# Eight expert tiles of gates to a memory row, in place of four, in a two-layer attention and expert kernel

## The chip, the cores and the metric

The kernel runs on one core of a Trainium2 chip. The metric is the device time of one execution in microseconds (us). TensorE is PE in the rows, its weight loads PEld, VectorE is DVE, ScalarE is ACT, GpSimd is POOL, and SyncE, which only issues transfers here, is SP.

## The reference

Two layers over 512 tokens of width 1024, all in float32: attention with compressed keys and values in the first, a gated linear recurrence in the second, and after each a mixture of 16384 small experts. The change lies in the experts, which are, for each block of 128 tokens:

```python
q = (xt @ w_q).reshape(PEER_TBLOCK, PEER_HEADS, 2, PEER_HALF)
s = jnp.einsum('thpd,hpnd->thpn', q, sub_keys).astype(jnp.float32)
s1, i1 = lax.top_k(s[:, :, 0], PEER_TOPK)
s2, i2 = lax.top_k(s[:, :, 1], PEER_TOPK)
...
top, pos = lax.top_k(cand, PEER_TOPK)
eidx = jnp.take_along_axis(cidx, pos, axis=-1)
gates = jax.nn.softmax(top, axis=-1)
act = jax.nn.gelu(jnp.einsum('td,thkd->thk', xt, u[eidx]).astype(jnp.float32), approximate=False)
return jnp.einsum('thk,thkd->td', (gates * act).astype(xt.dtype), v[eidx])
```

Every token takes 128 experts (8 heads, 16 each) out of 128 x 128.

## The kernel before

**Dense and gathered tokens.** For 384 of the 512 tokens (`D`) the experts are computed densely: all 16384 of them, in 128 tiles of 128 experts, with a gate that is zero wherever a token did not choose the expert. For the last 128 tokens (`FAR`) the chosen rows of `u` and `v` are gathered one expert a token at a time: 128 gathers of 512 KB from `u` and 128 from `v` a layer, issued by GpSimd (line 616) into six buffers, and used by VectorE in `far_dot` (line 1337) and `far_add` (line 1353). A gather waits until the row six before it has been used.

**The u phase.** Step `s` of 0 to 127 multiplies tile `u[s]` with the tokens on TensorE: 24 matmuls of 384 columns (8 pieces of the width, each as three products of a high and a low part). ScalarE takes the bank through Gelu into one of four buffers `act_st` (line 849), and SP stores it into `acts_dram` (192 KB, line 545). Gelu of tile c waits until the store of tile c - 4 has landed. The four weight buffers are filled by SP (line 514), ScalarE rounds a tile to its high part (line 679), and VectorE makes the low part (line 1330). SP issues the load of a tile once the low part of the tile four before it is made.

**The gates.** From step 41 to 118 TensorE also makes the gates of the dense tokens from one-hot factors, four tokens (a quad) at a time. ScalarE moves them (line 857) into one of two buffers `gate_st` of 32 tokens each, and `store_gates` (line 550) writes such a buffer, 2 MB, into `gates_dram`: 12 stores a layer. The array in memory is `gates_dram[GG, P, HALVES, GF, HALF_TOK]`: `GF` expert tiles lie together, and a row that is stored in one piece holds `GF` tiles x 32 tokens. The last store of a layer goes out at about step 116.

**The v phase.** Step c of 0 to 127 multiplies the product of activation and gate with tile `v[c]`: 18 matmuls of 512 columns. SP loads the activations back (192 KB a tile, line 559), and the gates of `GF` tiles in one transfer, `load_gates` (line 565), into one of two buffers. VectorE multiplies both (`make_product`, line 1364), ScalarE rounds the product to its high part (line 875), VectorE makes its low part (`product_low`, line 1370), and TensorE waits for that.

**What sets the order.** The program is written by hand as one list for each engine, and each engine runs its list in order. All of SP's transfers go into one queue (q1), the gathers into another (q0). On SP the two first gate loads stand at step 127, ahead of the first four `v` tiles and of the stores of activations 120 to 127:

```python
                    if s == NKEYS - 1:
                        for b in range(2):
                            sp.wait_ge(gate_stored[b], 16 * (HALVES // 2) * (layer + 1))
                        load_gates(0)
                        load_gates(1)
                    for c in range(act_loads_before(s), act_loads_before(s + 1)):
                        if c % GF == 2 and 1 <= c // GF < GG - 1:
                            load_gates(c // GF + 1)
                        load_act(c)
```

On ScalarE `product_high(0)`, the step before TensorE's first `v` matmul, stands in step 125, behind `gelu(125)` and the rounding of tile `v[1]`. So the end of the u phase and the start of the v phase are linked through the landing of the store of activations 121.

Of the kernel before, what the change touches and what calls it, by code (L numbers as in the profile page):

```python
# [43 lines left out]
RING = 4  # L44
APART = 2
AFTER_VALUES = (TT - 1, *range(TT - 1))
GF = 4
GG = NKEYS // GF
DENSE_T = TT - 1
D = DENSE_T * P  # L50
# [90 lines left out]
def act_loads_before(step):  # L141


    return min(max(min(2 * (step - NKEYS + 3), ACTS_EARLY), step - NKEYS, 0), NKEYS)
# [161 lines left out]
def model(nc, x, pos, consts, masks, gains, fgain, frows, mla_t, hg_t, pq_t, keys_t, u_t, u_rows, v_t, out):  # L306
    jobs = plan()
    ctx = ExitStack()
    with ctx:
# [5 lines left out]
        def sem(name):  # L315
            if name not in sems:
                sems[name] = ctx.enter_context(nc.semaphore(name))
            return sems[name]


        acts_dram = nc.dram_tensor("acts_dram", [NKEYS, P, D], F32, kind="Internal").ap()
        gates_dram = nc.dram_tensor("gates_dram", [GG, P, HALVES, GF, HALF_TOK], F32, kind="Internal").ap()

# [29 lines left out]
        def cut(offset, *shape):  # L353
            n = int(np.prod(shape))
            ap = arena[:, offset:offset + n]
            if len(shape) == 1:
                return ap
            names = "abcd"[:len(shape)]
            return ap.rearrange(f"p ({' '.join(names)}) -> p {' '.join(names)}", **dict(zip(names, shape)))
# [15 lines left out]
        keysT = cut(0, 16, NKEYS)  # L375
        gate_st = cut(3072, 2, GG, GF, HALF_TOK)
        gate_ld = cut(3072, 2, HALVES, GF, HALF_TOK)
        cand = cut(3072, HEADS, STAIRS)
# [130 lines left out]
        def _(sp):  # L509
# [20 lines left out]
            def experts(layer):  # L530
# [30 lines left out]
                def load_gates(g):  # L561

                    if g >= 2:
                        sp.wait_ge(sem("product_made"), NKEYS * layer + GF * (g - 1))
                    sp.dma_start(gate_ld[:, g % 2].rearrange("p h f t -> p (h f t)"),
                                 gates_dram[g].rearrange("p h f t -> p (h f t)")).then_inc(gate_loaded[g % 2], 16)

                stored = 0
                for s in range(2 * NKEYS + 8):
# [14 lines left out]
# [3 lines that stand above are left out]
# [1436 lines left out]
```

## Time and profile before

| | us |
|---|---|
| median of 3 runs | 2978.71 |
| lowest and highest | 2976.94, 2978.97 |
| the profiled execution | 2975.47 |
| its span, first to last instruction | 2973.7 |
| TensorE busy | 2941.9 (99%) |
| VectorE busy | 2364.5 (80%) |
| ScalarE, GpSimd busy | 1197.0, 1284.2 |
| DMA | 799.76 MB, mean 269 GB/s |

The layers' expert phases take 325 to 1425 us and 1865 to 2960 us of the span. The granted TensorE clock has a mean of 0.997. The transfers are read in two ways: as the rate of a stretch (GB/s), and as the share that each queue's packets take of the 16 DMA engines. The share can exceed 100%, since packets of one engine overlap; so a cost is worked out from the rate. A chain of waits is followed back from the last instruction of a stretch to whatever released it, and its rows tell what sets the end of that stretch.

### The profile page before, as it was taken

How to read it: one execution, taken by the hardware profiler on the slowest of the kernel's cores; microseconds unless marked ns; L12 is line 12 of the kernel's file. 1: busy time of each engine (PE TensorE's matmuls, PEld its weight loads, DVE VectorE, ACT ScalarE, POOL GpSimd, SP SyncE). 2: the span in 40 equal slices, each digit the busy share in tenths (PEclk: the TensorE clock that was granted, in tenths of full speed). 3: DMA queues.
4: the chain of work that ended last, by engine and by line, in shares of the span. 5: the costliest groups of instructions: out<-in, count | busy, mean ns of one | idle time of the engine just before them, and what ended most of it. 6: DMA issues, size and time to landing. Idle time of an engine off the chain costs nothing.

```text
span 2973.7 us, 43852 instructions
## 1 busy us (share of the span) xinstructions
PE 2941.9 (99%) x16072; PEld 2620.6 (88%) x16072; DVE 2364.5 (80%) x4442; ACT 1197.0 (40%) x1881; POOL 1284.2 (43%) x747
## 2 busy tenths in 40 slices
PE   8999999999999999999999999999999999999999
PEld 7578999999998888888889888999999998888887
DVE  7547999899978888888256637999898968888887
ACT  5543333444433333333435633334444433333333
POOL 4133565434434444442447433655344444444441
PEclk9999999999999999999999999999999999999999
DMA  4022468999999999998221022559999999999995
GB/s 153 32 80 97 129 200 303 352 374 375 368 378 396 365 366 357 362 360 295 100 92 43 30 94 85 181 174 346 365 361 381 364 385 397 360 361 365 358 363 213
DMA packets 345572, 799.76 MB, mean 269 GB/s; under 512 B 27920, under 2 KB 192016, under 8 KB 345104
## 3 DMA queue, kind: packets, MB, share of 16 engines
q1 hardware_dynamic: 271488, 528.44, 50.7%
q0 software_dynamic: 73728, 268.47, 23.6%
q8 instruction: 129, 2.11, 0.3%
q14 instruction: 83, 0.68, 0.1%
q10 hardware_dynamic: 144, 0.07, 0.0%
HBM read 694.10 MB, written 102.76 MB: 268 GB/s over the span
## 4 chain that ended last, share of the span: by engine, by line
PE 96%; DVE 1%; ACT 1%; DMA 1%; issue 0%; POOL 0%; SPq 0%; DVEq 0%; ACTq 0%
PE PS L1583 29%; PE PS L1585 29%; PE PS L1584 29%; PE PS L1789 3%; PE PS L1860 1%; PE PS L1766 1%; PE PS L1697 1%; DMA acts_dram<-arena 1%; DVE resid L1086 1%; PE PS L1696 1%; PE PS L1743 1%; ACT arena L692 0%; PE PS L1731 0%; ACT w_hi L679 0%; POOL w_lo L605 0%
## 5 line engine op out<-in xcount | busy, mean ns | idle before, releaser
L679 ACT ACTIVATE w_hi<-w_raw 128x1024 fp32r<-128x1024 f32 x607 | 641.0, 1057 | 697.1 <-PE PS L1585 652.0
L1583 PE MATMUL PS<-x_hi,w_hi 128*128 128x384 f32 (+1 forms) x2596 | 910.4, 351 | 6.3 <-POOL w_lo L605 4.9
L1585 PE MATMUL PS<-x_hi,w_lo 128*128 128x384 f32 (+1 forms) x2596 | 899.3, 346 | 0.0
L1584 PE MATMUL PS<-x_lo,w_hi 128*128 128x384 f32 (+1 forms) x2596 | 897.9, 346 | 0.0
L1583 PE MATMUL PS<-w_hi,x_hi 128*128 128x512 f32 x1744 | 680.0, 390 | 1.6 <-DVE x_lo L1370 0.8
L1584 PE MATMUL PS<-w_lo,x_hi 128*128 128x512 f32 x1744 | 678.9, 389 | 0.0
L1585 PE MATMUL PS<-w_hi,x_lo 128*128 128x512 f32 x1744 | 678.8, 389 | 0.0
L616 POOL DMA_INDIRECT arena<-in_v_t,arena x256 | 428.6, 1674 | 557.1 <-DVE resid L1353 520.5
L605 POOL TENSOR_TENSOR w_lo<-w_raw,w_hi 128x1024 fp32r<-128x1024 f32 x167 | 412.6, 2474 | 536.4 <-ACT w_hi L679 536.3
L1330 DVE TENSOR_TENSOR w_lo<-w_raw,w_hi 128x1024 fp32r<-128x1024 f32 x440 | 537.1, 1221 | 101.6 <-ACT w_hi L679 98.4
L616 POOL DMA_INDIRECT arena<-in_u_rows,arena x256 | 373.4, 1458 | 499.9 <-DVE arena L1337 446.2
L1583 PEld LDWEIGHTS PS<-x_hi,w_hi 128*128 128x128 f32 x2596 | 487.9, 188 | 26.8 <-issue 6.3
L1585 PEld LDWEIGHTS PS<-x_hi,w_lo 128*128 128x128 f32 x2596 | 487.5, 188 | 22.4
L1584 PEld LDWEIGHTS PS<-x_lo,w_hi 128*128 128x128 f32 x2596 | 488.1, 188 | 19.2 <-issue 0.2
L849 ACT ACTIVATE arena<-PS 128x384 f32<-128x384 f32 x256 | 125.9, 492 | 692.5 <-PE PS L1585 495.2
L1583 PEld LDWEIGHTS PS<-w_hi,x_hi 128*128 128x128 f32 x1744 | 327.7, 188 | 71.0 <-issue 3.0
L1585 PEld LDWEIGHTS PS<-w_hi,x_lo 128*128 128x128 f32 x1744 | 327.7, 188 | 68.1
L1584 PEld LDWEIGHTS PS<-w_lo,x_hi 128*128 128x128 f32 x1744 | 327.7, 188 | 67.8
L1353 DVE SCALAR_TENSOR_TENSOR resid<-arena,resid 128x1024 f32<-128x1024 f32 x256 | 327.5, 1279 | 1.3
L1337 DVE SCALAR_TENSOR_TENSOR arena<-arena 128x1024 f32<-128x1024 f32 x256 | 307.2, 1219 | 0.4
L1370 DVE TENSOR_TENSOR x_lo<-arena,x_hi 128x384 fp32r<-128x384 f32 x256 | 144.7, 565 | 163.1 <-ACT x_hi L875 155.8
L1364 DVE TENSOR_TENSOR arena<-arena 128x384 f32<-128x384 f32 x256 | 141.3, 552 | 3.7 <-DMA arena<-acts_dram 3.7
(187 smaller groups left out, 2321.4 us busy)
## 6 DMA issues: line engine op xcount, KB each, us to landing
w_raw<-in_u_t SPq DMA_DIRECT2D x256, 512.0 KB
w_raw<-in_v_t SPq DMA_DIRECT2D x256, 512.0 KB
acts_dram<-arena SPq DMA_DIRECT2D x256, 192.0 KB
gates_dram<-arena SPq DMA_DIRECT2D x24, 2048.0 KB
arena<-acts_dram SPq DMA_DIRECT2D x256, 192.0 KB
arena<-gates_dram SPq DMA_DIRECT2D x64, 768.0 KB
w_raw<-in_hg_t SPq DMA_DIRECT2D x40, 512.0 KB
w_raw<-in_pq_t SPq DMA_DIRECT2D x32, 512.0 KB
```

Source lines behind the costliest of these rows:

```text
L605: pool.tensor_tensor(w_lo[:, n % RING, :], w_raw[:, n % RING, :], f32(w_hi[:, n % RING, :]), ALU.subtract).then_inc(pool_low, 1)
L616: pool.indirect_dma_start(row[k % ROWS], None, u_at if k < HK else v_at, bass.IndirectOffsetOnAxis(ap=at, axis=0))\
L679: act.activation(w_hi[:, slot, :], w_raw[:, slot, :], ACT.Copy).then_inc(hi_ready, 1)
L849: act.activation(act_st[:, c % RING, :], PS[:, c % 4, 0:D], ACT.Gelu).then_inc(gelu_done, 1)
L1330: dve.tensor_tensor(w_lo[:, n % RING, :], w_raw[:, n % RING, :], f32(w_hi[:, n % RING, :]), ALU.subtract).then_inc(dve_low, 1)
L1337: dve.scalar_tensor_tensor(r, r, 1.0, far_x, ALU.mult, ALU.mult, accum_out=far_act[:, k:k + 1]).then_inc(sem("dotted"), 1)
L1353: dve.scalar_tensor_tensor(resid[:, FAR, :], r, far_w[:, k:k + 1], resid[:, FAR, :], ALU.mult, ALU.add).then_inc(sem("far_added"), 1)
L1364: dve.tensor_tensor(product[:, c % RING, :].rearrange(tokens, t=HALF_TOK), act_ld[:, c % RING, :].rearrange(tokens, t=HALF_TOK), gate_ld[: ...
L1370: dve.tensor_tensor(product_at(x_lo, c), product[:, c % RING, :].rearrange("p (t n) -> p t n", n=P), product_at(f32(x_hi), c), ALU.subtrac ...
L1583: pe.matmul(ps, wh, xh, start=start, stop=False)
L1584: pe.matmul(ps, wh, xl, start=False, stop=False)
L1585: return pe.matmul(ps, wl, xh, start=False, stop=stop)
```

## The change

`GF` becomes 8, and so `GG` 16.

```diff
-GF = 4
+GF = 8
 GG = NKEYS // GF
```

A store of gates still moves 2 MB, now in 2048 rows of 1 KB in place of 4096 of 512 bytes. A load of gates brings 8 tiles: 1.5 MB in place of 768 KB, with 12 KB a partition in place of 6 KB, and there are 32 loads in place of 64. Each of the two load buffers grows from 1536 to 3072 words a partition; they lie over the store buffers, which are free by then. The loads that follow the first two stand every 8 tiles in place of every 4, six steps ahead of their first use in place of two. The lists of TensorE, VectorE, ScalarE and GpSimd have the same rows as before; only SP's differs.

SP's list at the end of the first layer's u phase, before (`w_raw` are the weight buffers, `arena` holds all others):

```order
L545 DMA acts_dram<-arena 128x384
L565 DMA arena<-gates_dram 128x1536 x2
L514 DMA w_raw<-in_v_t 128x1024
L545 DMA acts_dram<-arena 128x384
L514 DMA w_raw<-in_v_t 128x1024
L545 DMA acts_dram<-arena 128x384
```

And with the change:

```order
L545 DMA acts_dram<-arena 128x384
L565 DMA arena<-gates_dram 128x3072 x2
L514 DMA w_raw<-in_v_t 128x1024
L545 DMA acts_dram<-arena 128x384
L514 DMA w_raw<-in_v_t 128x1024
L545 DMA acts_dram<-arena 128x384
```

Nothing moved here, but the two transfers ahead of the `v` tiles and the stores are twice as large.

SP's list a few steps into the v phase, before:

```order
L565 DMA arena<-gates_dram 128x1536
L559 DMA arena<-acts_dram 128x384
L514 DMA w_raw<-in_v_t 128x1024
L545 DMA acts_dram<-arena 128x384
L559 DMA arena<-acts_dram 128x384
L514 DMA w_raw<-in_v_t 128x1024
L559 DMA arena<-acts_dram 128x384
L514 DMA w_raw<-in_v_t 128x1024
L559 DMA arena<-acts_dram 128x384
L514 DMA w_raw<-in_v_t 128x1024
L565 DMA arena<-gates_dram 128x1536
```

And with the change, from the load of activations 9 on:

```order
L559 DMA arena<-acts_dram 128x384
L514 DMA w_raw<-in_v_t 128x1024
L565 DMA arena<-gates_dram 128x3072
L559 DMA arena<-acts_dram 128x384
L514 DMA w_raw<-in_v_t 128x1024
L559 DMA arena<-acts_dram 128x384
L514 DMA w_raw<-in_v_t 128x1024
```

The load of gates that stood at tile 6 is gone, and one of twice its size stands where that of tile 10 was; the next follows eight tiles later.

## Rows read from the trace of the kernel before

**Rows 1.** The page: busy us and share of each engine, and the chain's shares

```profile
PE 2941.9 (99%) x16072; PEld 2620.6 (88%) x16072; DVE 2364.5 (80%) x4442; ACT 1197.0 (40%) x1881; POOL 1284.2 (43%) x747
PE 96%; DVE 1%; ACT 1%; DMA 1%; issue 0%; POOL 0%; SPq 0%; DVEq 0%; ACTq 0%
```

**Rows 2.** Who waited for whom, TensorE: us in total, times, longest

```profile
PE PS L1641 <- DVE arena L1056: 9.1, 3, 8.3
PE PS L1583 <- DVE x_lo L1370: 0.8, 1, 0.8
```

**Rows 3.** Chain of waits at the second layer's phase change: start, us, what

```profile
2427.88 13.19 DMA acts_dram<-arena
...
2441.54 1.05 ACT w_hi L679
2442.59 0.42 ACT x_hi L875
...
2443.03 0.57 DVE x_lo L1370
```

**Rows 4.** Timeline of the first layer's phase change: ScalarE, VectorE, TensorE

```profile
899.38 0.49 ACT L849 ACTIVATE arena<-PS 128x384 f32<-128x384 f32 x1 [2.80 <-DMA acts_dram<-arena]
900.71 0.51 ACT L875 ACTIVATE x_hi<-arena 128x384 fp32r<-128x384 f32 x1
901.26 0.56 DVE L1370 TENSOR_TENSOR x_lo<-arena,x_hi 128x384 fp32r<-128x384 f32 x1 [3.43 <-ACT x_hi L875]
901.75 0.34 PE L1585 MATMUL PS<-x_hi,w_lo 128*128 128x384 f32 x1
901.96 0.47 PE L1583 MATMUL PS<-w_hi,x_hi 128*128 128x512 f32 x1
```

**Rows 5.** SP's timeline, second layer: gate store, tile behind it, gate loads

```profile
2400.06 0.37 SPq L550 DMA_DIRECT2D gates_dram<-arena  x1
2400.47 13.15 SPq L514 DMA_DIRECT2D w_raw<-in_u_t  x1
...
2419.27 0.89 SPq L565 DMA_DIRECT2D arena<-gates_dram  x2
```

**Rows 6.** By stretch: us, busy us of each engine, granted clock, DMA share, GB/s

```profile
882.00:892.00 10.00, 10.00 (x59) 10.00 (x59) 9.10 (x14) 2.92 (x5) 7.63 (x5) 1.00 1.03 415
2434.00:2444.00 10.00, 9.19 (x53) 8.90 (x52) 2.98 (x6) 3.29 (x5) 2.54 (x2) 1.00 1.03 413
2485.00:2940.00 455.00, 455.00 (x2009) 376.87 (x2008) 382.56 (x455) 164.92 (x224) 190.96 (x114) 1.00 0.97 360
```

**Rows 7.** Transfers of 885 to 886.5 us, nearly all a load of gates

```profile
DMA packets 120, 0.64 MB, mean 430 GB/s; under 512 B 14, under 2 KB 15, under 8 KB 120
```

**Rows 8.** Transfers of 867 to 868 us, all of them a store of gates

```profile
DMA packets 677, 0.35 MB, mean 347 GB/s; under 512 B 0, under 2 KB 677, under 8 KB 677
```

**Rows 9.** Queues of 2430 to 2441 us: packets, MB, share of 16 engines

```profile
q0 software_dynamic: 676, 2.51, 55.8%
q1 hardware_dynamic: 812, 2.04, 46.8%
```

**Rows 10.** Gathers' queue in 899 to 903 us, then in 2441 to 2445 us

```profile
q0 software_dynamic: 94, 0.32, 19.6%
...
q0 software_dynamic: 187, 0.64, 39.2%
```

**Rows 11.** ScalarE and VectorE at the first load of gates within the v phase

```profile
923.40 1.06 ACT L679 ACTIVATE w_hi<-w_raw 128x1024 fp32r<-128x1024 f32 x1 [5.75 <-DMA w_raw<-in_v_t]
...
915.90 0.55 DVE L1364 TENSOR_TENSOR arena<-arena 128x384 f32<-128x384 f32 x1
...
920.66 0.56 DVE L1364 TENSOR_TENSOR arena<-arena 128x384 f32<-128x384 f32 x1 [1.18 <-DMA arena<-acts_dram]
...
924.90 0.56 DVE L1370 TENSOR_TENSOR x_lo<-arena,x_hi 128x384 fp32r<-128x384 f32 x1 [1.36 <-ACT x_hi L875]
925.38 0.56 DVE L1364 TENSOR_TENSOR arena<-arena 128x384 f32<-128x384 f32 x1
```

## The prediction, on record before the change was run

> **What bounds the kernel now.** I read the page first. TensorE is busy for 99% of the span, and the chain that ended last is 96% TensorE [rows 1]. An edit that touches only SP's transfers can therefore act in two ways alone: it removes one of TensorE's few waits, or it makes a new one. The list of TensorE's waits says how much there is to remove: the largest entry belongs to the norms, and the only one that hangs on the gates or activations is a single wait of 0.8 us for the low part of a product [rows 2]. So the gain has a ceiling of about 1 us, whatever the change does for the transfers. The rest of the question is where a slower or later transfer would reach TensorE.
>
> The second view is the chain of waits around that one wait. It stands at the change from the u phase to the v phase of the second layer, and the reader is to see its largest link: the store of activations 121, issued at 2427.88 us, lands 13.19 us later; then come the rounding of the tile `v[1]` (1.05 us), `product_high(0)` and `product_low(0)`, and then TensorE's first `v` matmul [rows 3]. A store of 192 KB does not need 13 us by itself: it stands in a queue. In the first layer the same sequence ends just in time. Gelu of tile 125 starts at 899.38 us after a wait for a store, `product_high(0)` at 900.71, `product_low(0)` runs from 901.26 to 901.82, and TensorE, whose last u matmul starts at 901.75, starts the `v` matmuls at 901.96 [rows 4]. At the 0.17 us from one u matmul to the next (59 in 10 us [rows 6]) 901.92 would have been possible, and the low part was ready at 901.82: about 0.1 us of slack. So in both layers the landing of that store sets the start of the v phase, with 0.1 us and no slack.
>
> The third view is the table by stretches. From the last store of gates to the start of the v phase the DMA engines are full: shares of 1.03 and 413 to 415 GB/s [rows 6]. In such a stretch every byte that is put ahead of the store delays it.
>
> **The change part by part.**
>
> *Larger first loads.* On SP the two first gate loads are issued at 2419.27 us [rows 5], ahead of the store of activations 121, in one queue. They grow from 2 x 0.786 MB to 2 x 1.573 MB. While such a load had the engines nearly alone it ran at 430 GB/s [rows 7], so the 1.573 MB that come on top take 1.573 / 0.430 = 3.7 us a layer. They bring the gates of tiles 8 to 15, which nobody wants for another 30 us. At the 413 GB/s of the full stretch [rows 6] it would be 3.8; I take 3.7, since the two ends lie so close.
>
> *Larger rows of the stores.* In a stretch that holds nothing but 512-byte rows the rate is 347 GB/s [rows 8]. The 2.097 MB of a store take 6.0 us at that rate, and would take 4.9 us at the 430 GB/s of the large rows [rows 7]. No row shows 1 KB; so the saving lies between 0 and 1.1 us a store. If the difference is a fixed cost per packet, it halves when the packets halve, and half of 1.1 us, some 0.5 us, is my value. Of the 12 stores of a layer only the last one counts: TensorE waited for none of the others, and it stands ahead of the critical store in the same full queue. So -0.5 us a layer (0 to -1.1).
>
> The Trainium skill, page "DMA: Bandwidth & Descriptors", section "Specifications", gives 512 B as the smallest transfer that reaches line rate; by that rule alone the longer rows save nothing, and the sum below would be 1 us higher. The trace does not agree: 347 against 430 GB/s [rows 7, 8].
>
> *The gathers take their turns.* The queue of the gathers runs beside SP's. From 2430 to 2441 us it took 55.8% of the engines, and SP's queue 46.8% [rows 9]: while gathers are pending, SP's transfers get less than half. But there are only six gathers in flight until VectorE has used the next row, and VectorE is held there by `product_low(0)` itself. What of them had not run when the critical store landed, can now run before it: 0.32 MB after 899 us in the first layer and 0.64 MB after 2441 us in the second [rows 10], which is 0.8 and 1.5 us at 415 GB/s [rows 6]. The bound below is nothing, if the store keeps its place ahead of them. With shares of 56 to 47 the extra 3.2 us of SP's queue leave room for all of it, so I take 0.8 and 1.5.
>
> The same page, section "Queues, rings and completion order", says that each DMA engine goes round-robin between the queues that have work for it. By that rule the full amounts hold, and the shares of [rows 9] agree with it; without it the sum would be 2.3 us lower.
>
> *SP is free earlier.* Behind the last store of gates SP needs 13.15 us to issue one weight tile [rows 5]; half as many descriptors should shorten that. I cost it at nothing, because the transfers behind it go through a queue that is never empty from there on: an earlier place at the issuing end changes no landing. If it did, the first rival below would hold.
>
> *The later loads.* Half as many loads, twice the size, six steps ahead of use in place of two. The first one within the v phase moves from tile 6 to tile 10. In the profile the one at tile 6 has cost VectorE's cadence: the products start 4.8 and 4.7 us apart there (915.90, 920.66, 925.38), where TensorE takes 4.08 us a tile (455 us over 2009 matmuls, 18 a tile [rows 6]), and ScalarE waited 5.75 us for a weight tile [rows 11]. TensorE did not wait. Its tile 6 was due at 901.96 + 6 x 4.08 = 926.4 us, and the low part of that product was ready at 925.5 [rows 4, 11]. Without this load the margin can grow for four more tiles at the pace of the other steps. So the move is worth nothing to TensorE, and the doubled load at tile 10 meets a larger margin; I cost it at 0, with an upper bound in the second rival. Over the rest of the phase the bytes are the same, at 360 GB/s against the 430 that the engines reach.
>
> *The sum.* First layer: 3.7 - 0.5 + 0.8 = 4.0 us later for the critical store, less 0.1 us of slack, 3.9. Second layer: 3.7 - 0.5 + 1.5 = 4.7, all of it a wait, since there the 0.8 us stand already. Behind the store nothing changes. 3.9 + 4.7 = +8.6 us. The profiled execution took 2975.47 us, so it would take 2984.1; the median of the runs shown is 3.2 us above the profiled one, and the forecast on that scale is 2978.71 + 8.6 = 2987.3, say **2987 us**. The step needs TensorE's two waits at the phase change to be worth their length alone, and the clock to stay: it is granted at 1.00 in the stretch with the wait of 0.8 us [rows 6].
>
> The unknown terms give this case a range of its own: all low (stores save 1.1, no gathers) 3.9 - 0.6 - 0.8 = 2.5 and 4.7 - 0.6 - 1.5 = 2.6, so +5.1; all high (stores save nothing) +9.6. That is 2984 to 2988.
>
> **The rivals.**
>
> *The landing is bound by issue, not by bytes.* If the long block on SP is what makes the stores of activations 116 and onward late, halving the descriptors shortens the block from 13.15 to about 6.6 us, more than the 3.7 us that the loads add. Then the critical store lands no later, and the 0.8 us wait goes away. For it speaks the size of the block [rows 5]; against it speak the full engines in every later stretch [rows 6]. It decides if the engines show gaps between the last gate store and the first gate load. The time would be 2975.5 - 0.8, or 2978 on the scale of the median, and at the most 2 us above it: not slower.
>
> *Bytes only.* The store keeps its place against the gathers. Then the sum is 3.7 - 0.5 - 0.1 + 3.7 - 0.5 = +6.3 us, 2985, and with cheaper 1 KB rows +5.1. The shares of [rows 9] speak against it.
>
> *The bursts stall TensorE as well.* The load at tile 6 cost about 1.5 us of margin (4.8 and 4.7 us in place of 4.08, twice). One of twice the size costs 3 us and, with the gathers' turns, up to 6; the margin at tile 10 will be some 4 to 6 us. If it is short, 1 to 2 us a layer come on top, and if it recurs at tile 18 the same again: +10.5 to +16, say 2991. For it speaks the wait of 5.75 us [rows 11]; against it the steady phase with 0.97 share and no wait on TensorE [rows 2, 6].
>
> That the change does not do what it says can be left out: SP's list shows it.
>
> **How the numbers follow.** The forecast has 0.57, the bound by issue 0.17, bytes only 0.14, the bursts 0.12. A measurement of this kernel can tell about 0.2%, 6 us, from no change. The forecast's own range begins at +5.1, so 0.10 of its 0.57 count as within 6 us; of the bound by issue 0.14 do, and 0.03 count as faster, for a gain that I have not seen; of bytes only 0.08 do. Slower by over 0.2%: 0.47 + 0.06 + 0.12 = 0.65. Within 0.2%: 0.10 + 0.14 + 0.08 = 0.32. Faster: 0.03. The range leaves out most of the bound by issue below and the worst bursts above: 2979.5 to 2993.
>
> **What would show it.** TensorE's waits: the entry for the low part of a product (line 1370) should stand at two waits, near 4 and 5.5 us, in place of one of 0.8. The chain before each should hold a store of activations that lands some 16 to 18 us after its issue. SP's block behind a gate store should be shorter with no effect on TensorE, and the rate within a gate store should rise from 347 to about 380 GB/s. In the v phase TensorE should have no wait. The forecast is wrong if Gelu of tile 125 starts within 1 us of its place relative to TensorE's last u matmul, if the gathers run only after the store, or if waits appear at tiles 11 or 12.

## The result, and the profile after

The changed kernel takes 2985.49 us in the median of 10 runs (2982.04 to 2987.59), the kernel before 2977.49 us (2972.51 to 2979.97). The ratio is 1.0024, with a 95% interval of 1.0015 to 1.0033: slower by 8.0 us, where +8.6 was forecast. The profiled execution has a span of 2985.0 us, against 2973.7. These two lie further apart than the medians: the changed kernel's took 2986.81 us, and that of the kernel before, with 2975.47 us, was the fastest of its three.

The list of TensorE's waits, after (us in total, times, longest); the second row answers to the same one in [rows 2]:

```profile
PE PS L1641 <- DVE arena L1056: 9.1, 3, 8.3
PE PS L1583 <- DVE x_lo L1370: 8.1, 2, 4.3
```

The wait for the low part of product 0 was one of 0.8 us, and is two of 3.8 and 4.3. The chain of waits before the second one (start, us, what) answers to [rows 3]:

```profile
2428.64 21.01 DMA acts_dram<-arena
...
2450.11 1.05 ACT w_hi L679
2451.16 0.42 ACT x_hi L875
...
2451.60 0.57 DVE x_lo L1370
```

The links behind the store have the lengths that they had; the store of activations 121 lands 21.0 us after its issue in place of 13.2. Counted from the issue of the last gate store, it was issued 3.1 us sooner (24.8 in place of 27.8 us) and landed 4.8 us later (45.8 in place of 41.0). SP's timeline over the same change of phase, second layer, answers to [rows 5]:

```profile
2403.88 0.37 SPq L550 DMA_DIRECT2D gates_dram<-arena  x1
2404.29 6.73 SPq L514 DMA_DIRECT2D w_raw<-in_u_t  x1
...
2419.55 2.75 SPq L565 DMA_DIRECT2D arena<-gates_dram  x2
```

SP is held for 6.7 us behind the gate store in place of 13.2, and that has not helped. What decides is seen when all bytes are counted from the issue of the last gate store to the start of Gelu of tile 125, which waits for the critical store. Second layer, before (2400.1 to 2441.2 us) and after (2403.9 to 2449.7): all transfers, and SP's queue alone.

```profile
DMA packets 8821, 16.28 MB, mean 396 GB/s; under 512 B 530, under 2 KB 6014, under 8 KB 8819
...
q1 hardware_dynamic: 7102, 9.96, 65.2%
```

```profile
DMA packets 6955, 18.49 MB, mean 404 GB/s; under 512 B 557, under 2 KB 3991, under 8 KB 6697
...
q1 hardware_dynamic: 5079, 11.64, 64.8%
```

A mean rate is bytes over time, so that the two fit together proves nothing by itself. What the count shows is that the engines were no slower in the longer stretch (404 GB/s in place of 396): it is longer because more bytes passed in it. The 2.21 MB more would take 5.6 us at 396 GB/s, and the higher rate gives 0.9 us of them back: 4.7 us. Of the 2.21 MB, SP's queue carries 1.68, of which 1.57 are the larger first loads, and the gathers' queue 0.54 (6.28 and 6.82 MB). The first layer, from 857.9 to 899.4 us before and from 859.1 to 904.5 us after, shows the same in sum:

```profile
DMA packets 8737, 16.25 MB, mean 392 GB/s; under 512 B 520, under 2 KB 5898, under 8 KB 8734
DMA packets 6960, 18.49 MB, mean 407 GB/s; under 512 B 564, under 2 KB 3998, under 8 KB 6701
```

There the 2.24 MB more would be 5.7 us, and the higher rate gives 1.7 back.

There is a second thing in the profile that the prediction had not reckoned with. The stretches at both changes of phase, after (columns as in [rows 6]; the granted clock stands third from the end):

```profile
904.00:909.00 5.00, 1.89 (x7) 1.56 (x8) 2.60 (x5) 4.06 (x8) 0.16 (x1) 0.95 0.99 387
909.00:914.00 5.00, 5.00 (x17) 4.00 (x16) 5.00 (x9) 2.35 (x4) 3.20 (x2) 0.71 0.70 225
2447.00:2452.00 5.00, 1.05 (x7) 0.73 (x5) 1.58 (x2) 2.27 (x5) 0.00 (x0) 0.93 1.04 413
2452.00:2459.00 7.00, 6.69 (x17) 5.36 (x18) 7.00 (x12) 3.20 (x5) 3.36 (x2) 0.56 0.71 236
2459.00:2465.00 6.00, 6.00 (x28) 4.94 (x27) 6.00 (x9) 2.98 (x5) 3.04 (x3) 1.00 1.01 338
```

Right behind each wait the granted clock falls from 2.4 to 1.2 GHz for part of the stretch: from 2452 to 2459 us TensorE starts 17 matmuls in 7 us, where 28 fit into the 6 us after. At the level of the last row, 7 us hold 33, so this stretch lost about 3.4 us of work, and the one at 909 us about 1.4 (17 matmuls in 5 us, where 23 would fit). In the profile the change thus costs 7.3 us of waits and some 5 us of half clock, together somewhat more than the 11.3 us between the spans; the half clock that both kernels have in other stretches is not the same in the two executions either.

### The profile page after: what moved, and what is told of

It reads as the page before. It is cut to its first block, busy times and chain, and to the rows that moved or that the text cites. A ratio compares the mean times of both kernels' runs of the same rounds, so it can differ in the third digit from the quotient of the medians.

```text
span 2985.0 us, 43820 instructions
## 1 busy us (share of the span) xinstructions
PE 2946.8 (99%) x16072; PEld 2624.1 (88%) x16072; DVE 2365.9 (79%) x4442; ACT 1196.8 (40%) x1881; POOL 1256.4 (42%) x747
## 4 chain that ended last, share of the span: by engine, by line
PE 94%; DMA 2%; DVE 1%; ACT 1%; issue 0%; POOL 0%; SPq 0%; DVEq 0%; ACTq 0%
PE PS L1583 28%; PE PS L1585 28%; PE PS L1584 28%; PE PS L1789 3%; DMA acts_dram<-arena 2%; PE PS L1860 1%; PE PS L1766 1%; PE PS L1697 1%; DVE resid L1086 1%; PE PS L1696 1%; PE PS L1743 1%; ACT arena L692 0%; PE PS L1731 0%; ACT w_hi L679 0%; PE PS L1887 0%
## 5 line engine op out<-in xcount | busy, mean ns | idle before, releaser
L616 POOL DMA_INDIRECT arena<-in_u_rows,arena x256 | 346.9, 1355 | 519.5 <-DVE arena L1337 468.5
```

Source lines behind the costliest of these rows:

```text
L616: pool.indirect_dma_start(row[k % ROWS], None, u_at if k < HK else v_at, bass.IndirectOffsetOnAxis(ap=at, axis=0))\
```

## The experiments

The times of one version spread by 4 to 14 us, and those of the kernel before by 13 to 20 in a group of runs. Each ratio is to the kernel before on the same chip. Where an edit adds lines, the line numbers shift by 1 to 6.

**The second load later.** From the changed kernel:

```diff
                         load_gates(0)
+                    if s == NKEYS + 3:
                         load_gates(1)
```

> The changed kernel, with the second of the two first gate loads issued three steps later, behind the stores of activations 120 to 123. My theory (the change costs what the bytes ahead of the critical store take in a full queue): ahead of that store now stands one load of 1.57 MB, as many bytes as two loads did before the change, and the last gate store is some 0.5 us shorter. So TensorE's wait for the low part of a product falls from 8.1 us in two waits to at most 0.5 us in all, no stretch at half clock stands behind the phase change, and the ratio to the kernel before is 0.9995 to 1.0002. Rival (the larger loads cost by themselves, wherever they stand: 12 KB packets, or the later bursts of 1.5 MB): the waits stay at 4 us or more and the ratio at 1.002 or above.

2974.64 us, ratio 0.998 (0.9971 to 0.9989). TensorE has no wait for a product in the profile. The same count of bytes as above, for this kernel, 2399.3 to 2438.6 us of the second layer:

```profile
DMA packets 6515, 15.81 MB, mean 402 GB/s; under 512 B 510, under 2 KB 3954, under 8 KB 6385
...
q1 hardware_dynamic: 4923, 10.00, 65.5%
```

SP's queue has 1.64 MB fewer than the changed kernel, the gathers 1.0 MB fewer (5.78 against 6.82), at about the same rate, and the stretch is 39.3 us long. The rival falls: the larger loads cost nothing by themselves, only where they stand. I had forecast 0.9995 to 1.0002; the kernel is faster than that, and than the kernel before beyond the interval; a second profile of the kernel before (the last experiment) shows a part of what it had to gain.

**The same edit to the kernel before:**

> The kernel before, with only the second first gate load (768 KB) issued three steps later. My theory: 0.79 MB fewer ahead of the critical store, 1.8 us, which takes away the wait of 0.8 us in the second layer and leaves TensorE about 1 us of slack at both phase changes. No wait on the low part of a product, ratio 0.9995 to 1.0000. Rival (the phase change is set by the issue on SP or by the gate store alone): the wait of 0.8 us stays.

2975.50 us, ratio 0.9986 (0.9976 to 0.9995). No wait for a product, as expected. The gain is larger than the 0.9995 to 1.0000 that was forecast, here too. It has other waits, though, 2.1 us at the gates' matmuls.

**The loads without the stores.** Memory as before (`GF` = 4), but each load takes two groups:

```diff
-                    sp.dma_start(gate_ld[:, g % 2].rearrange("p h f t -> p (h f t)"),
-                                 gates_dram[g].rearrange("p h f t -> p (h f t)")).then_inc(gate_loaded[g % 2], 16)
+                    sp.dma_start(gate_ld[:, 2 * b:2 * b + 2].rearrange("p g h f t -> p g (h f t)"),
+                                 gates_dram[2 * g:2 * g + 2].rearrange("g p h f t -> p g (h f t)"))\
+                        .then_inc(gate_loaded[b], 16)
```

> The loads of the change without its stores: the gates lie in memory as before (rows of 512 bytes stored), and each load brings two groups of four tiles, 1.5 MB with two pieces of 6 KB a partition, at the same places in SP's list as in the changed kernel. My theory: the same bytes ahead of the critical store, and a gate store that is 0.5 us longer in each layer, so the two waits sum to 8.5 to 10 us and the ratio is 1.0025 to 1.0035. Rival (the 12 KB rows of the loads, or the 1 KB rows of the stores, are what costs): waits below 4 us and a ratio below 1.0015.

2990.85 us, ratio 1.0036 (1.0023 to 1.0049). The wait, and the bytes from 2406.5 to 2454.6 us:

```profile
PE PS L1587 <- DVE x_lo L1374: 13.0, 2, 6.5
```

```profile
DMA packets 9431, 18.90 MB, mean 393 GB/s; under 512 B 579, under 2 KB 6147, under 8 KB 9428
...
q1 hardware_dynamic: 7546, 12.02, 66.4%
```

So the loads alone bring more waits than the whole change does, 13.0 against 8.1 us, where I had expected 8.5 to 10. The intervals of the two ratios overlap (1.0015 to 1.0033 for the change), but the same pair with the gathers held (below) is apart beyond its intervals. The longer rows of the stores thus give back about 5 us of waits, where I had put 0.5 us a layer on them. One other thing differs between the two kernels, the pieces of the loads, 6 KB here and 12 KB in the changed kernel. While they moved beside gathers the rates were 430 GB/s (2436 to 2438 us here) and 436 (2431 to 2435 us of the changed kernel), which is 0.1 us over the 3.15 MB of two loads. The rate during a store is what I took it for: one microsecond that holds nothing but 1 KB rows (2414 to 2415 us of the changed kernel) ran at 386 GB/s, between the 347 and 430 of [rows 7, 8], which makes 6.0 - 5.4 = 0.6 us a store.

```profile
DMA packets 377, 0.39 MB, mean 386 GB/s; under 512 B 0, under 2 KB 377, under 8 KB 377
```

The rest of the gap is taken up below.

**The gathers held.** From the changed kernel, on GpSimd ahead of the first gather of `v` rows:

```diff
+                    if k == HK:
+                        pool.wait_ge(sem("product_low"), NKEYS * layer + 1)
                     at = row_at[:, k % HK:k % HK + 1]
```

> The changed kernel, with the first gather of a v row of each layer (and with it all later ones) held until the low part of product 0 is made. It tests the term for the gathers' turns. If three of the six gathers beside the critical store no longer run before it, it lands up to 3 x 1.26 = 3.8 us earlier, and at the least the 0.8 and 1.5 us of my sum come back: the two waits sum to 1 to 6 us, the ratio is 1.0005 to 1.0018. Rival (SP's queue keeps its place, the gathers take nothing from it): the waits stay at 8.1 us. The held gathers might make VectorE late for the rows behind the phase change; TensorE has 4 us a tile there, and I expect no wait from it.

2975.85 us, ratio 0.998 (0.9971 to 0.9990). The waits for the low parts are four, 1.4 us in all, as expected (1 to 6 us); the ratio is better than the 1.0005 to 1.0018 forecast, as with the second load late. From 2399.2 to 2441.2 us:

```profile
DMA packets 6517, 16.90 MB, mean 402 GB/s; under 512 B 508, under 2 KB 3939, under 8 KB 6259
...
q1 hardware_dynamic: 5070, 11.62, 70.5%
```

SP's queue carries what it does in the changed kernel (11.62 and 11.64 MB), and the gathers 5.25 in place of 6.82 MB. The difference is 1.57 MB, three gathers of 0.524 MB: those that were held. At 402 GB/s that is 3.9 us, and the stretch is 3.8 us shorter. In the changed kernel three gathers of `v` rows were issued at 2433.3, 2438.3 and 2440.3 us, while the critical store stood in its queue (2428.6 to 2449.7 us). All three had run ahead of it, so the gathers' turns are as real as I assumed them, and a gather that runs early costs its full length.

**The changed kernel again,** beside the next three:

> The changed kernel once more, on the same chip as the three runs of this group, for comparison with them and for a second profile: the times of single executions spread over 5 to 14 us. If the wait at the phase change is what the change costs, the two waits for the low part of product 0 should again sum to 6 to 10 us, with a stretch at half the granted clock behind each, and the ratio to the kernel before should be 1.0015 to 1.003.

2984.32 us (2981.84 to 2990.02), ratio 1.0016 (1.0007 to 1.0025). Two waits, 8.2 us, and again a granted clock of 0.58 and 0.56 in the 7 us behind them.

**Both edits together:**

> The changed kernel with both: the second first gate load three steps later, and the gathers of v rows held until the low part of product 0. Each alone has brought TensorE's waits at the phase change from 8.1 to 0 and 1.4 us and the time to 0.998 of the kernel before. My theory: with no wait left to remove, the two do not add up; ratio 0.9975 to 0.9990, the low part of product 0 done 2 us or more earlier than with either, and no half clock there. Rival (each removes a cost of its own elsewhere, say in the bursts of the v phase): the gains add up to 0.997 or less.

2974.60 us, ratio 0.9986 (0.9977 to 0.9994). No wait, and no gain beyond either edit alone: the low part of product 0 is ready 4 us earlier than with the gathers held alone, and 1 to 2 us earlier than with the second load late alone (2 or more were expected), and TensorE has no use for it.

**The wait filled.** Into TensorE's list between the last u tile and the first v tile:

```diff
+                for _ in range(15):
+                    pe.matmul(PS[:, 7, 0:P], ident, iota, start=True, stop=True)
```

> The changed kernel, with 15 small float32 matmuls of constants (3 to 4 us, into a bank that the first v matmul overwrites) put into TensorE's list between the last u tile and the first v tile, where it waits 3.8 and 4.3 us. Theory of the clock: the half clock seen right behind these waits (3.4 and 6.8 us long, some 5 us of time) comes from TensorE's idle time before it; with the wait filled it does not occur, the fill costs nothing as long as it is shorter than the wait, and the time falls by 2 to 5 us against the changed kernel, ratio 1.000 to 1.0015. Rival (the clock falls there for another reason, or at random): the half clock stays behind the phase changes and the time is that of the changed kernel or up to 2 us above it, ratio 1.002 to 1.0035.

2983.84 us (2980.45 to 2984.32), ratio 1.0016 (1.0007 to 1.0025). The stretches of the phase changes in its profile, first and second layer:

```profile
904.00:908.00 4.00, 4.00 (x35) 3.85 (x33) 0.58 (x2) 1.95 (x4) 0.00 (x0) 1.00 1.04 410
908.00:914.00 6.00, 5.67 (x26) 4.67 (x26) 6.00 (x10) 4.67 (x7) 2.35 (x2) 1.00 0.71 245
2447.00:2451.00 4.00, 4.00 (x35) 4.00 (x34) 0.98 (x1) 1.48 (x3) 0.00 (x0) 1.00 1.03 410
2451.00:2458.00 7.00, 6.38 (x31) 5.22 (x30) 6.60 (x12) 5.18 (x9) 2.62 (x2) 1.00 0.72 258
```

With the wait filled by work that nobody needs, the clock stays at 2.4 GHz, so in the profile the half clock does come from TensorE's idle time. The spans differ by 6.2 us (2982.0, against 2988.2 for the changed kernel of this group), but the latter is that of the slowest of its 11 executions. The medians are only 0.5 us apart, where I had expected 2 to 5, and the ratios are the same. What the fill changes is the upper end, 2984.3 in place of 2990.0. The mean granted clock of each execution says more than one profile: it is 0.997 or above in all 11 with the fill, and 0.995 or 0.996 in 5 of 11 without it, and these 5 are the slowest, 2984.5 us and more. Over the 11 the clock averages 0.9971 and 0.9964, which is 2.1 us of 2984 (an estimate, from clocks given to three digits), and the mean times are 2983.0 and 2984.8 us. So the half clock costs about 2 us on average, not 5, though with this spread the times alone do not show it. The third kernel of the group fits: the kernel with both edits, which has no wait, has a mean of 2974.6 us, 8.4 us below the filled kernel, and TensorE's waits or their fill are 8.2 us.

**The double loads with the gathers held.** It asks where the 5 us between the two layouts come from.

> The loads of the change without its stores (rows of 512 bytes as before), with the gathers of v rows held until the low part of product 0. Without the hold this kernel waited 13.0 us in the two phase changes and the changed kernel 8.1 us: 2.4 us a layer apart, where the rates inside a gate store account for 0.6. If the other 1.8 us are gathers that come in ahead because everything is later (theory A), then with the gathers held the low part of product 0 is ready only about 0.6 us later than with the change's stores and held gathers (44.4 to 44.8 us after the issue of the last gate store there, so 45 to 45.5 here), and the two waits sum to 1.5 to 3 us, ratio 0.9980 to 0.9993. If they come from the longer block on SP behind a store of 4096 rows (theory B), the 2.4 us a layer stay: ready at 46.5 to 47.5 us, waits of 5 to 7 us in all, ratio 0.9995 to 1.001.

2986.28 us, ratio 1.0021 (1.0009 to 1.0033). Waits of 5.9 us for the low part, which was ready 45.6 and 46.3 us after the issue of the gate store; in the first layer that store was itself issued 2.1 us later against TensorE's tiles. The waits are those of theory B, the block on SP; the times from the store's issue lie between the two theories, and the ratio is above both. The twin with 1 KB rows, the changed kernel with the gathers held, had 0.998 (0.9971 to 0.9990) and 1.4 us of waits, so the rows of the stores do matter here, beyond the intervals. Theory B went to a test of its own.

**SP held, no byte moved.** From the changed kernel:

```diff
-                    sp.wait_ge(gelu_done, NKEYS * layer + 4 + c + 1)
+                    sp.wait_ge(gelu_done, NKEYS * layer + 4 + (119 if c == 116 else c) + 1)
```

> The changed kernel, with SP held for some 4 to 5 us behind the last gate store of each layer: it issues the store of activations 116 only after Gelu of tile 119 in place of 116, 11.4 us after the issue of the gate store in place of 6.8. No byte is added or moved in the order of the queue; this gives SP about the block that it has behind a store of 512-byte rows. Theory B (SP's block is a term of its own: what SP issues later lands later, because in the meantime the gathers have the engines): the low part of product 0 is ready 1.5 to 4 us later than the 48.1 us after the gate store's issue of the changed kernel, the two waits sum to 11 to 15 us, the ratio is 1.0025 to 1.005. Theory of the full queue, as in my prediction: no landing changes, 48 to 48.6 us, waits of 8 to 9 us, ratio as the changed kernel, 1.0015 to 1.0025.

2983.63 us, ratio 1.0014 (1.0005 to 1.0023). SP's timeline shows that it was held: store 116 goes out 11.5 us after the gate store in place of 7.2.

```profile
2403.52 0.37 SPq L550 DMA_DIRECT2D gates_dram<-arena  x1
2403.93 6.33 SPq L514 DMA_DIRECT2D w_raw<-in_u_t  x1
2414.97 0.32 SPq L545 DMA_DIRECT2D acts_dram<-arena  x1
```

The bytes from 2403.5 to 2449.4 us are those of the changed kernel, 18.49 MB at 403 GB/s, Gelu of tile 125 starts 45.5 and 45.9 us after the gate store's issue (45.4 and 45.8 in the changed kernel), and the two waits sum to 8.2 us. So in this kernel the hold moves no landing, and the first rival of the prediction falls with it. The reason is not that SP's queue never empties. From 2416 to 2419 us, behind the hold, it moved 0.29 MB in place of 0.61, but the gathers took the engines meanwhile, and the rate was 409 GB/s (420 in the changed kernel).

For the kernels with 512-byte rows theory B is not ruled out in full. Their 5 us are in the two counts: the one with double loads moved 18.90 MB at 393 GB/s, the changed one 18.49 at 404. That is 48.1 - 45.8 = 2.3 us in the second layer, 1.3 of it the lower rate and 1.0 the 0.4 MB. The rate within a store accounts for 0.6 us. Another 0.7 us lie in the three microseconds right behind the store, 2419 to 2422 us, where SP's queue ran low and the gathers did not fill the engines:

```profile
DMA packets 256, 0.92 MB, mean 306 GB/s; under 512 B 19, under 2 KB 34, under 8 KB 256
...
q1 hardware_dynamic: 84, 0.28, 25.5%
```

At 404 GB/s these three would have moved 1.21 MB. The same dip stands at this place in the double loads with the gathers held (330 GB/s from 2422 to 2425 us), and none in the changed kernel. Whether the longer block on SP causes it was not tested.

**The small rows where nothing waits.** The kernel before with the second load later and the gathers held, to be set against the same two edits on the changed kernel:

> The kernel before (4 tiles a row, 768 KB loads) with the second first gate load three steps later and the gathers of v rows held. It tells what the 1 KB rows are worth where nothing waits at the phase change: the same kernel with the change's layout had 2974.6 us. If the rows of 512 bytes cost only engine time that is hidden, both are the same within 1 us and as even; if they cost TensorE an occasional wait in the u phase (two executions of kernels with such rows had 2.1 and 3.5 us of waits at the gates' matmuls, none with 1 KB rows had), this one is 0.5 to 2 us slower in the median and spreads further up, beyond 2978. Ratio 0.9980 to 0.9995.

2977.57 us (2972.09 to 2982.18), ratio 0.9994 (0.9984 to 1.0004), against 0.9986 (0.9977 to 0.9994) for the twin with 1 KB rows: in the expected direction, with intervals that overlap. It has 1.4 us of waits at the gates' matmuls.

**The kernel before again:**

> The kernel before once more, for a second profile. Its 35 executions beside the last group of runs spread from 2973.6 to 2993.3 us, and the profiled one of my prediction was among the fastest; so a typical one should show more waits of TensorE than the 0.8 us for the low part of product 0: 1 to 4 us there in one or both layers, or at the gates' matmuls of the u phase.

2978.95 us, a span of 2977.2. TensorE's waits:

```profile
PE PS L1583 <- DVE x_lo L1370: 2.2, 2, 1.9
PE PS L1789 <- issue: 1.5, 3, 0.9
```

Here the kernel before waits at both changes of phase (0.4 and 1.9 us), and three times at the gates' matmuls (line 1789) in the u phases. Waits of the latter kind appear in four of the six profiles of kernels with 512-byte rows (1.4 to 3.5 us), and in none of the seven with 1 KB rows.

## Why the prediction was right, point by point

**The ceiling.** It holds for the profiled execution, and not for the kernel. A second execution shows 3.7 us of waits in the kernel before, so the profile that I read was one of its better ones. Edits that merely clear the phase change beat the kernel before by 0.14 to 0.20%, 3 to 5 us in the medians. The 3.7 us of that one execution are of this size; how the waits vary from one execution to the next is not shown.

**The place.** Right: the critical chain is the one named, with the same links behind the store, and each edit to the changed kernel that took bytes from in front of the store of activations 121 brought the waits from 8.1 us to 1.4 or to nothing.

**Larger first loads, +3.7 us a layer.** Right. In the second layer SP's queue carried 1.68 MB more before the critical store, and moving one load away took 1.64 MB out again and the whole wait with it. In the first layer it carried 2.03 MB more (9.58 and 11.61), 0.46 beyond the loads; what these were is not settled.

**Larger rows of the stores, -0.5 us a layer.** The rate was right (386 GB/s for 1 KB, 0.6 us), the size of the term was not. Over the whole stretch the change raised the rate by more than the store alone does, which was worth 1.7 us in the first layer and 0.9 in the second, and without the long rows the change cost 5 us more of waits. The step "only the last one counts" does not hold either: in the u phase small rows go with occasional waits of TensorE at the gates' matmuls, and with a late last store: in the execution of [rows 5] the next Gelu follows its issue after 1.3 us, in the changed kernel after 2.6, so the store had gone out 1.3 us later against TensorE's tiles.

**The gathers' turns, +0.8 and +1.5 us.** Right in kind; the gathers carried 0.22 MB more in the first layer (6.62 and 6.84) and 0.54 in the second, 0.5 and 1.3 us. The Trainium skill's rule of turns between the queues (page "DMA: Bandwidth & Descriptors", section "Queues, rings and completion order") agrees with the trace: all three gathers that were issued while the critical store stood in its queue ran before it.

**SP free earlier, 0.** Right, and tested: SP's block halved, and holding it for 4 us longer changed no landing. The reason that the prediction gave, engines that are full from the last gate store on, is too strong. [rows 6] begin 24 us and more behind that store; the first microseconds behind it ran at less in the kernel before as well, 352 GB/s from 858 to 863 us, and in the second layer:

```profile
2400.00:2404.00 4.00, 4.00 (x25) 4.00 (x24) 1.65 (x4) 1.47 (x3) 1.09 (x2) 1.00 0.99 331
```

And the sign "lands 16 to 18 us after its issue" was missed, 21.0 us in the second layer, since the issue came sooner; an issue time says little in a full queue, and the landing counted from the gate store is as summed.

**The later loads, 0.** Right. The waits for the low part are two, both at product 0; ScalarE's waits for a `v` tile, before and after, show that the bursts did not grow worse:

```profile
ACT w_hi L679 <- DMA w_raw<-in_v_t: 42.6, 18, 5.8
ACT w_hi L679 <- DMA w_raw<-in_v_t: 11.9, 4, 4.1
```

The later loads alone do not bring this fall: with the second first load late they stand at the same places, and the waits are 68.9 us, and cost TensorE nothing either.

**The sum.** Gelu of tile 125 came 3.9 us later in the first layer and 4.7 us later in the second, from the issue of the last gate store on (41.5 to 45.4, and 41.1 to 45.8), which are the 4.0 and 4.7 of the sum. The terms beneath are off in both directions, more bytes and a higher rate than forecast, so that the sums meet this closely is in part luck. TensorE's second wait is 4.3 and not 5.5 us, because the gate store itself came 1.3 us earlier against TensorE's tiles. The half clock was missing in the sum: "the clock to stay" was taken from a wait of 0.8 us, and does not hold for one of 4. That the total came out at 8.0 for 8.6 is partly luck as well: the waits differ by 7.3 us between the two first profiles, and by 4.4 between the changed kernel and the second profile of the kernel before (8.1 less 2.2 and 1.5). The half clock adds about 3 us to that: the clocks of the changed kernel's second group average 0.9964, those of the kernel before beside it 0.9974.

## What to carry to other kernels

Where the DMA engines are full, as here, what moves a landing is the bytes put ahead of it, in its own queue and in the others; count them from the trace between two events, and move whatever is not needed yet behind what is waited for. A larger transfer is no saving if half of its contents stand ahead of something urgent. And read more than one profile of a kernel whose runs spread: the waits that come and go are what an edit can remove.

## What the runs showed of the hardware

- Rows of 512 bytes, 1 KB and 6 KB between the core and its memory moved at 347, 386 and 430 GB/s.
- SP is held in issuing the transfer behind one of many rows: 10 to 14 us behind 4096 rows, 6.2 to 7.2 us behind 2048. In the kernel with 2048 rows, a hold of 4 us more cost nothing, while the gathers kept the engines at 409 GB/s.
- Behind idle times of TensorE of 2.3 to 6.5 us its granted clock fell to 1.2 GHz for part of the next 5 to 7 us, at both phase changes in all five profiles that have such waits (mean clock there 0.56 to 0.76); it stayed at 2.4 GHz behind waits of up to 1.9 us, and with the waits filled by 15 small matmuls. The Trainium skill, page "TensorE: Matmul & The Clock Gate", section "Part 1: The HAM clock gate (the "warmup" mystery)", has the clock follow how busy TensorE has been; the trace agrees.
